# A three-block network on one core: the inverse roots of five norms are multiplied onto the matmuls' outputs, and the raw residual is fed to them tile by tile

## The chip, the cores and the metric

One core of one Trainium2 chip runs the whole network in one program. The metric is the time of one execution in device microseconds, lower is better. The engines are TensorE (PE in the views), VectorE (DVE), ScalarE (ACT), GpSimd (POOL) and SyncE (SP, which starts the transfers of weights).

## The reference

The network works on 256 tokens of width 1024 in float32; its first block prepends 16 meta tokens (272 columns). Block one: a conformer convolution (pw1, gate, depthwise convolution, layer norm, SiLU, pw2) and a SwiGLU FFN of width 2816. Block two: a pooling mix and a mixture of eight experts. Block three, twice a layer: a hybrid attention layer (input projection `w_in2`, gates, output `wo2`), then a recurrent layer (`w_in3`, `wo3`) and a second FFN. Ahead of each matmul stage stands a norm:

```python
def rms_norm(x, g):
    xf = x.astype(jnp.float32)
    y = xf * lax.rsqrt(jnp.mean(xf * xf, axis=-1, keepdims=True) + RMS_EPS)
    return y.astype(x.dtype) * g
...
def swiglu(h, w_gate, w_up, w_down):
    return (jax.nn.silu(h @ w_gate) * (h @ w_up)) @ w_down
```

The inverse root is one number per token, so it may stand before the matmul or behind it, as long as the step behind (SiLU, sigmoid) sees the scaled value.

## The kernel before

Activations lie feature-major: eight tiles of 128 features by 256 or 272 tokens. Weights come in chunks of 1 MB ([128, 2048], eight blocks of 128x256) into a ring of six slots. A float32 product is made of three: ScalarE copies a chunk to a rounded high part (L969), VectorE subtracts to get the low part (L1220), and inputs are split the same way (high on ScalarE, L989; low on VectorE, L1227). `split_pair` (L443) then issues, for each of the eight input tiles and both halves, high by high (L455), high by low (L458) and low by high (L459): 48 matmuls fill two banks of PSUM, called a pair here. Three pairs of banks go round; `bank_owner` makes TensorE wait until the values of three pairs ago have been taken out. Chunks are split three ahead of their use.

Each engine runs its own list in the order in which the code issues it, and waits on counting semaphores; nothing reorders it. ScalarE's split of a chunk waits until TensorE has begun on an earlier one (`pre_begun`, `post_begun`).

The norms are numbered 0 to 10: 0 before pw1, 1 the layer norm, 2 before FFN 0 (22 pairs, then 4 down pairs), 3 before the pooling, 4 before the router, 5 (the network's middle norm, `final_g`) and 6 before `w_in2` (24 pairs), 7 behind `wo2`, 8 before `w_in3` (21 pairs), 9 before FFN 3 (22 and 4 pairs), 10 the last one. In a norm ScalarE squares the tiles (L979), TensorE sums them over the features by a matmul with ones (`sum_squares`, L483), VectorE scales the sum and adds epsilon (L1206), ScalarE takes the root (L981), VectorE the reciprocal (`rstd`, L1209), and then VectorE, ScalarE and VectorE again make scaled input, high and low part tile by tile (L1241, L989, L1227). In the FFN, ScalarE takes SiLU of the gate's bank into `gate_sb` (L1022) and VectorE multiplies it by the other bank. In `w_in2` and `w_in3` some pairs are taken by VectorE (L1496), others by ScalarE with their function. The 24 gates per token (L703) follow pair 23 of `w_in2` and the compression (L714) follows them. GpSimd builds diagonals for the convolution (L1799) in the first 120 us and makes a few adds of 128x256 late in the program (L1804).

## Time and profile before

| | us |
|---|---|
| median of 3 runs | 2279.29 |
| lowest and highest run | 2275.84, 2280.2 |
| the profiled execution | 2278.21 |
| its span | 2276.2 |
| TensorE busy | 2134.3 (94%) |
| VectorE, ScalarE, GpSimd busy | 1522.6, 1174.8, 120.6 |
| mean granted clock of TensorE | 0.951 |

The span runs from the first to the last instruction recorded, 2 us less than the execution's time. The granted clock is given as a share of 2.4 GHz; 0.50 is the level of 1.2 GHz. A busy share is a mean over all stages.

### The profile page before, as it was taken

How to read it: one execution, taken by the hardware profiler on the slowest of the kernel's cores; microseconds unless marked ns; L12 is line 12 of the kernel's file. 1: busy time of each engine (PE TensorE's matmuls, PEld its weight loads, DVE VectorE, ACT ScalarE, POOL GpSimd, SP SyncE). 2: the span in 40 equal slices, each digit the busy share in tenths (PEclk: the TensorE clock that was granted, in tenths of full speed). 3: DMA queues.
4: the chain of work that ended last, by engine and by line, in shares of the span. 5: the costliest groups of instructions: out<-in, count | busy, mean ns of one | idle time of the engine just before them, and what ended most of it. 6: DMA issues, size and time to landing. Idle time of an engine off the chain costs nothing.

```text
span 2276.2 us, 31696 instructions
## 1 busy us (share of the span) xinstructions
PE 2134.3 (94%) x12296; PEld 1869.2 (82%) x12296; DVE 1522.6 (67%) x1697; ACT 1174.8 (52%) x1223; POOL 120.6 (5%) x170
## 2 busy tenths in 40 slices
PE   7989999699999999999999999989998899779998
PEld 6979998588888888878888888789976799658997
DVE  7865543689897988889797988864254365325553
ACT  4134432367777776777777777644243243404442
POOL 8800000000000000000000000000000000020000
PEclk9989999799999999999999999999857999889999
DMA  4214444089898989989898989835401345124541
GB/s 180 91 61 144 180 172 147 20 338 371 314 369 326 357 338 346 347 337 370 315 368 327 356 336 347 312 127 186 169 1 38 111 151 188 51 93 148 186 180 61
DMA packets 70101, 504.18 MB, mean 222 GB/s; under 512 B 7680, under 2 KB 8704, under 8 KB 8832
## 3 DMA queue, kind: packets, MB, share of 16 engines
q1 hardware_dynamic: 70016, 502.95, 59.0%
q8 instruction: 65, 1.06, 0.2%
q14 instruction: 20, 0.16, 0.0%
HBM read 501.87 MB, written 1.05 MB: 221 GB/s over the span
## 4 chain that ended last, share of the span: by engine, by line
PE 86%; DVE 7%; ACT 3%; issue 3%; DMA 0%; POOL 0%; DVEq 0%; ACTq 0%; POOLq 0%
PE ps L455 10%; PE ps L459 10%; PE ps L458 10%; PE ps L629 8%; PE ps L625 8%; PE ps L628 8%; PE ps L650 5%; PE ps L654 4%; PE ps L653 4%; PE ps L437 3%; PE ps L501 2%; PE ps L483 2%; DVE ring_r L1403 1%; PE ps L586 1%; PE ps L592 1%
## 5 line engine op out<-in xcount | busy, mean ns | idle before, releaser
L1403 DVE TENSOR_TENSOR ring_r<-ring,high 128x2048 fp32r<-128x2048 f32 x227 | 517.7, 2289 | 96.7 <-ACT high L1062 91.6
L455 PE MATMUL ps<-sq_r,high 128*128 128x256 f32 (+1 forms) x1472 | 422.4, 287 | 26.1 <-DVE scr_r L1227 26.1
L458 PE MATMUL ps<-scr_r,high 128*128 128x256 f32 (+1 forms) x1536 | 440.5, 287 | 0.0
L1062 ACT ACTIVATE high<-ring 128x2048 fp32r<-128x2048 f32 x224 | 428.5, 1913 | 18.9 <-DMA ring<-w_stream 18.6
L459 PE MATMUL ps<-sq_r,ring_r 128*128 128x256 f32 (+1 forms) x1472 | 421.1, 286 | 0.0
L1220 DVE TENSOR_TENSOR ring_r<-ring,high 128x2048 fp32r<-128x2048 f32 x120 | 274.9, 2293 | 213.7 <-ACT high L969 213.4
L628 PE MATMUL ps<-ring_r,big_r 128*128 128x512 f32 x896 | 350.0, 391 | 0.0
L969 ACT ACTIVATE high<-ring 128x2048 fp32r<-128x2048 f32 x120 | 228.8, 1909 | 153.2 <-PE ps L455 153.0
L455 PEld LDWEIGHTS ps<-sq_r,high 128*128 128x128 f32 x1472 | 281.1, 191 | 28.8 <-issue 26.5
L458 PEld LDWEIGHTS ps<-scr_r,high 128*128 128x128 f32 x1536 | 294.9, 192 | 0.2
L625 PE MATMUL ps<-high,big_r 128*128 128x512 f32 x704 | 287.2, 408 | 4.2 <-DVE ring_r L1403 4.2
L459 PEld LDWEIGHTS ps<-sq_r,ring_r 128*128 128x128 f32 x1472 | 281.6, 191 | 0.0
L629 PE MATMUL ps<-high,big_r 128*128 128x512 f32 x704 | 275.9, 392 | 0.0
L1403 DVE TENSOR_TENSOR ring_r<-ring,scr_r 128x2048 fp32r<-128x2048 f32 x112 | 254.7, 2289 | 8.0 <-ACT scr_r L1062 3.6
L1062 ACT ACTIVATE scr_r<-ring 128x2048 fp32r<-128x2048 f32 x112 | 214.3, 1914 | 16.0 <-DMA ring<-w_stream 15.5
L628 PEld LDWEIGHTS ps<-ring_r,big_r 128*128 128x128 f32 x896 | 169.1, 189 | 32.1
L653 PE MATMUL ps<-ring_r,big_r 128*128 128x512 f32 x448 | 174.5, 389 | 0.0
L625 PEld LDWEIGHTS ps<-high,big_r 128*128 128x128 f32 x704 | 132.7, 188 | 28.6 <-DVE ring_r L1403 4.4
L629 PEld LDWEIGHTS ps<-high,big_r 128*128 128x128 f32 x704 | 132.4, 188 | 28.4
L1066 ACT ACTIVATE big_r<-ps 128x256 fp32r<-128x256 f32 x112 | 43.1, 384 | 161.5 <-PE ps L636 160.9
L650 PE MATMUL ps<-scr_r,big_r 128*128 128x512 f32 x256 | 102.4, 400 | 1.6
L455 PE MATMUL ps<-big_r,high 128*128 128x272 f32 (+1 forms) x352 | 100.7, 286 | 2.0 <-ACT gate_sb L1022 2.0
(344 smaller groups left out, 3179.6 us busy)
## 6 DMA issues: line engine op xcount, KB each, us to landing
ring<-w_stream SPq DMA_DIRECT2D x477, 1024.0 KB, 4.8
h<-h_in SPq DMA_DIRECT2D x1, 1088.0 KB, 5.3
out<-hn SPq DMA_DIRECT2D x1, 1024.0 KB, 4.7
vec<-vec_in SPq DMA_DIRECT2D x1, 576.0 KB, 8.2
```

Source lines behind the costliest of these rows:

```text
L455: mm = pe.matmul(o, w_high[:, cols], x_high[:, k, 0:t], start=(k == 0), stop=False)
L458: pe.matmul(o, w_high[:, cols], x_low[:, k, 0:t], start=False, stop=False)
L459: mm = pe.matmul(o, w_low[:, cols], x_high[:, k, 0:t], start=False, stop=(k == kt - 1))
L625: mm = pe.matmul(o, x_item_high[:, k, :], w_high[:, cols], start=(k == 0), stop=False)
L628: pe.matmul(o, x_item_high[:, k, :], w_low[:, cols], start=False, stop=False)
L629: mm = pe.matmul(o, x_item_low[:, k, :], w_high[:, cols], start=False, stop=(k == KD - 1))
L650: mm = pe.matmul(o, hid_t_high[:, kk, :], w_high[:, cols], start=first, stop=False)
L653: pe.matmul(o, hid_t_high[:, kk, :], w_low[:, cols], start=False, stop=False)
L969: act.activation(parts_at(c, 0, CH)[0], blocks_at(c, 0, CH), ACT.Copy).then_inc(S["weights_high"], 1)
L1062: act.activation(w_high, w, ACT.Copy).then_inc(S["moe_high"], 1)
L1220: dve.tensor_tensor(w_low, blocks_at(c, 0, CH), w_high.bitcast(F32), ALU.subtract).then_inc(S["weights_low"], 1)
L1403: dve.tensor_tensor(w_low, w, w_high.bitcast(F32), ALU.subtract).then_inc(S["moe_low"], 1)
```

## The change

Norms 2, 5 with 6, 8 and 9 no longer scale the input by `rstd`. ScalarE copies the raw residual times the norm's weight (a pointer operand) as the high part, VectorE makes the low part in one instruction (`input_low`), and the pair of matmuls may start as soon as the first tile's parts are there. The sum of squares is issued behind pair 0 (norms 2, 8, 9) or pair 1 (norms 5, 6). Each pair's output is multiplied by `rstd` on VectorE on its way out of PSUM, and ScalarE's SiLU and sigmoids then work in place in SBUF. For the pairs whose output is token-major, two tiny matmuls turn `rstd` into a column (`turn_root`). Norms 5 and 6 share one input with the weights `gain56` = `final_g` x `pre_g`; the root of both together comes from two sums in the halves of bank 7, and `x` itself is scaled by VectorE in pairs 4 to 11.

In every norm but 0, GpSimd adds squares 0 to 5 (`sum_six`, five dependent adds), so that TensorE sums three tiles. ScalarE takes the root straight from PSUM with scale and epsilon; a small root ahead of it brings the table in. The gates and the `w_if` rows read the raw `x` with weights that GpSimd scales once; the gates move behind pair 2. The addition of the attention layer's output to `x` moves from VectorE to GpSimd. The FFN's pairs use the banks turned by one. Line numbers in the changed kernel differ: L473, L476, L477 are the three matmuls, L507 the sum of squares, L1002 and L1293 the two splits of weights.

```diff
-            def sum_squares(i, t):
-                for k in range(KD):
-                    pe.wait_ge(S["sq_ready"], 8 * i + k + 1)
-                    mm = pe.matmul(ps[:, 7, 0:t], ones[:, 0:P], sq[:, k, 0:t], start=(k == 0), stop=(k == KD - 1))
+            def sum_squares(i, t, bank=7, at=0):
+
+                if i == 0:
+                    tiles = range(KD)
+                else:
+                    tiles = (0, 6, 7)
+                    pe.wait_ge(S["sq_summed"], i)
+                for k in tiles:
+                    pe.wait_ge(*sq_at(i, k))
+                    mm = pe.matmul(ps[:, bank, at:at + t], ones[:, 0:P], squares_of(i)[:, k, 0:t],
+                                   start=(k == 0), stop=(k == KD - 1))
                 mm.then_inc(S["sum_done"], 1)
+
+            def turn_root(n):
+                pe.wait_ge(S["root_ready"], n + 1)
+                for t in range(2):
+                    mm = pe.matmul(ps[:, 6, 48 + t:49 + t], rstd[0:1, t * P:(t + 1) * P], ones[0:1, 0:1],
+                                   start=True, stop=True)
+                mm.then_inc(S["root_turned"], 1)
...
-                sum_squares(norm_i, t)
                 for p in range(KF):
-                    b = 2 * (p % 3)
-                    split_pair(b_in + p * KD, KD, in_high, x_low, t, b, S["ffn_gu"],
+                    b = 2 * ((p + 1) % 3)
+                    split_pair(b_in + p * KD, KD, sq_r, x_low, t, b, S["ffn_gu"],
                                after_split(split_n) if p == 0 else None)
-                    bank_owner[b] = (S["ffn_sig"], n * KF + p + 1)
-                    bank_owner[b + 1] = (S["ffn_mul"], n * KF + p + 1)
+                    bank_owner[b] = bank_owner[b + 1] = (S["ffn_scaled"], n * KF + p + 1)
+                    if p == 0:
+                        sum_squares(norm_i, t)
...
-                    b = 2 * (j % 3)
+                    b = 2 * ((j + 2) % 3)
...
-            pe.wait_ge(S["moe_all"], 1)
-
-
-            sum_squares(5, SEQ)
-            sum_squares(6, SEQ)
             for p in range(24):
                 b = 2 * (p % 3)
                 if p < 21:
-                    split_pair(BOFF["w_in2"] + p * KD, KD, in_high, in_low, SEQ, b, S["in2_done"],
+                    split_pair(BOFF["w_in2"] + p * KD, KD, hn_r, in_low, SEQ, b, S["in2_done"],
                                after_split(3) if p == 0 else None)
                 else:
 
-                    token_pair(BOFF["w_in2"] + p * KD, in_high, in_low, b, S["in2_done"])
-                bank_owner[b] = bank_owner[b + 1] = taken(taker2, "in2", p)
-
-            for t in range(2):
-                for k in range(KD):
-                    mm = pe.matmul(ps[:, 6, t * 24:(t + 1) * 24], hn256[:, k, t * P:(t + 1) * P],
-                                   vcol("w_gates", k * 24, 24), start=(k == 0), stop=(k == KD - 1))
-            mm.then_inc(S["gl_done"], 1)
-
-            pe.wait_ge(S["in2_act"], taker2.count("act"))
-            pe.wait_ge(S["in2_dve"], taker2.count("dve"))
+                    token_pair(BOFF["w_in2"] + p * KD, hn_r, in_low, b, S["in2_done"])
+                bank_owner[b] = bank_owner[b + 1] = (S["in2_dve"], p + 1)
+                if p == 1:
+                    sum_squares(5, SEQ)
+                    sum_squares(6, SEQ, at=SEQ)
+                if p == 2:
+                    for t in range(2):
+                        for k in range(KD):
+                            mm = pe.matmul(ps[:, 6, t * 24:(t + 1) * 24], x[:, k, t * P:(t + 1) * P],
+                                           vcol("w_gates", k * 24, 24), start=(k == 0), stop=(k == KD - 1))
+                    mm.then_inc(S["gl_done"], 1)
+                    turn_root(0)
...
+            def root(n_sums, t, eps, bank=7, at=0):
+
+                act.wait_ge(S["sum_done"], n_sums)
+                act.activation(var[:, 0:t], ps[:, bank, at:at + t], ACT.Sqrt, bias=eps, scale=1.0 / D)\
+                   .then_inc(S["std_ready"], 1)
+
+            def norm(i, src, t, ready, first_block=None, eps=eps_col, bank=7):
+
+                for k in range(KD):
+                    if first_block and k in (4, 6):
+                        split_weights(first_block // CH + k - 4)
+                    if k == KD - 2:
+                        act.activation(warm, eps_col, ACT.Sqrt)
+                    ready(k)
+                    act.activation(sq[:, k, 0:t], src[:, k, 0:t], ACT.Square).then_inc(S["sq_ready"], 1)
+                root(i + 1, t, eps, bank)
...
+            def input_parts(i, src, dst, gain, t, ready, first_block):
 
                 for k in range(KD):
                     if first_block and k in (4, 6):
                         split_weights(first_block // CH + k - 4)
                     ready(k)
-                    act.activation(sq[:, k, 0:t], src[:, k, 0:t], ACT.Square).then_inc(S["sq_ready"], 1)
-                act.wait_ge(S["var_ready"], i + 1)
-                act.activation(var[:, 0:t], var[:, 0:t], ACT.Sqrt).then_inc(S["std_ready"], 1)
-                if first_block == 0:
-                    split_weights(0)
-                if split_n is not None:
-                    for k in range(KD):
-                        if first_block == 0 and k == 3:
-                            split_weights(1)
-                        act.wait_ge(S["normed"], 8 * i + k + 1)
-                        act.activation(in_high[:, k, 0:t], hn[:, k, 0:t], ACT.Copy).then_inc(S["input_high"], 1)
-
+                    act.activation(dst[:, k, 0:t], src[:, k, 0:t], ACT.Copy, scale=gain[:, k:k + 1])\
+                       .then_inc(S["input_high"], 1)
+                    for q in (k,) if k < 6 else (6, 7) if k == 7 else ():
+                        act.activation(squares_of(i)[:, q, 0:t], src[:, q, 0:t], ACT.Square)\
...
+            input_parts(2, h, sq_r, vcol("ffn_g0", 0, 8), T0, lambda k: act.wait_ge(S["h1_ready"], k + 1),
+                        BOFF["ffn0_in"])
...
-                        act.wait_ge(S["ffn_gu"], n * 2 * KF + 2 * p + 2)
-                        if p >= 2:
-                            act.wait_ge(S["ffn_hid"], n * KF + p - 1)
-                        act.activation(gate_sb[:, p % 2, 0:t], ps[:, 2 * (p % 3), 0:t], ACT.Silu)\
+                        act.wait_ge(S["ffn_scaled"], n * KF + p + 1)
+                        act.activation(gu[:, p % 2, 0, 0:t], gu[:, p % 2, 0, 0:t], ACT.Silu)\
...
+            act.wait_ge(S["sq_summed"], 1)
+            for k in range(KD):
+                act.wait_ge(S["moe_out"], items * 4 + (k // 2 + 1))
+                act.activation(hn_r[:, k, 0:SEQ], x[:, k, :], ACT.Copy, scale=gain56[:, k:k + 1])\
+                   .then_inc(S["input_high"], 1)
+            for k in range(KD):
+                act.activation(sq[:, k, 0:SEQ], x[:, k, :], ACT.Square).then_inc(S["sq_ready"], 1)
+            for k in range(KD):
+                act.activation(squares2[:, k, 0:SEQ], x[:, k, :], ACT.Square, scale=vcol("final_g", k))\
+                   .then_inc(S["sq_ready"], 1)
+            act.wait_ge(S["var_ready"], 1)
+            act.activation(var[:, 0:SEQ], var[:, 0:SEQ], ACT.Sqrt).then_inc(S["std_ready"], 1)
+            act.wait_ge(S["root_ready"], 1)
+            root(7, SEQ, eps_col)
...
-            def inverse_root(i, t, eps):
-                dve.wait_ge(S["sum_done"], i + 1)
-                dve.tensor_scalar(var[:, 0:t], ps[:, 7, 0:t], 1.0 / D, eps, ALU.mult, ALU.add)\
-                   .then_inc(S["var_ready"], 1)
+            def inverse_root(i, t):
                 dve.wait_ge(S["std_ready"], i + 1)
...
+            def times_root(t):
+
+                return rstd[:, 0:t].unsqueeze(1).broadcast_to([P, 2, t])
...
+            def input_low(src, k, gain, t, high_part, low):
+
+                inputs_split[0] += 1
+                dve.wait_ge(S["input_high"], inputs_split[0])
+                dve.scalar_tensor_tensor(out=low[:, k, 0:t], in0=src[:, k, 0:t], scalar=gain[:, k:k + 1],
+                                         in1=high_part[:, k, 0:t].bitcast(F32), op0=ALU.mult, op1=ALU.subtract)\
+                   .then_inc(S["input_low"], 1)
...
+                if m in (4, 6):
+                    split_weights(BOFF["ffn0_in"] // CH + m - 4)
+                if m:
+                    input_low(h, m - 1, vcol("ffn_g0", 0, 8), T0, sq_r, in_low_ffn0)
+            input_low(h, KD - 1, vcol("ffn_g0", 0, 8), T0, sq_r, in_low_ffn0)
...
+                        b = 2 * ((p + 1) % 3)
+                        dve.wait_ge(S["ffn_gu"], n * 2 * KF + 2 * p + 2)
+                        if p >= 2:
+                            dve.wait_ge(S["ffn_hid"], n * KF + p - 1)
+                        dve.tensor_tensor(gu[:, p % 2, :, 0:t], ps[:, b:b + 2, 0:t], times_root(t), ALU.mult)\
+                           .then_inc(S["ffn_scaled"], 1)
                         split_weights((b_in + p * KD + KD - 1) // CH + LOOK)
                         dve.wait_ge(S["ffn_sig"], n * KF + p + 1)
-                        dve.tensor_tensor(gate_sb[:, p % 2, 0:t], ps[:, 2 * (p % 3) + 1, 0:t],
-                                          gate_sb[:, p % 2, 0:t], ALU.mult).then_inc(S["ffn_mul"], 1)
+                        dve.tensor_tensor(gu[:, p % 2, 1, 0:t], gu[:, p % 2, 0, 0:t], gu[:, p % 2, 1, 0:t], ALU.mult)\
+                           .then_inc(S["ffn_mul"], 1)
...
+                for k in (2 * n - 2, 2 * n - 1):
+                    if n:
+                        input_low(x, k, gain56, SEQ, hn_r, in_low)
+            for k in (6, 7):
+                input_low(x, k, gain56, SEQ, hn_r, in_low)
+            split_weights(BOFF["w_in2"] // CH + LOOK)
...
+                    ins = dve.scalar_tensor_tensor(out=dst, in0=ps[:, b:b + 2, 0:SEQ],
+                                                   scalar=0.125 if n < KS or QB <= n < KB else 1.0,
+                                                   in1=times_root(SEQ), op0=ALU.mult, op1=ALU.mult)
...
+                if k >= 2:
+                    input_low(x, k - 2, vcol("mix3_g", 0, 8), SEQ, hn_r, in_low)
...
+            def sum_six(i, t):
+
+                sums = squares_of(i)
+                pool.wait_ge(*sq_at(i, 0))
+                for k in range(1, 6):
+                    pool.wait_ge(*sq_at(i, k))
+                    ins = pool.tensor_tensor(sums[:, 0, 0:t], sums[:, 0, 0:t], sums[:, k, 0:t], ALU.add)
+                    if k < 5:
+                        step(ins)
+                ins.then_inc(S["sq_summed"], 1)
...
+            for i, t in ((1, T0), (2, T0), (3, T0), (4, SEQ), (5, SEQ), (6, SEQ)):
+                sum_six(i, t)
...
+            sum_six(7, SEQ)
+            for k in range(KD):
+                pool.wait_ge(S["post_scaled"], k + 1)
+                pool.tensor_tensor(x[:, k, :], x[:, k, :], zo[:, k, :], ALU.add).then_inc(S["normed"], 1)
+            sum_six(8, SEQ)
```

On VectorE at the end of pw2, before (`h<-ps` are the residual adds, `ring_r` the low part of weights, L1209 the reciprocal of norm 2):

```order
L1220 TENSOR_TENSOR ring_r<-ring,high 128x2048 [waits weights_high]
L1293 SCALAR_TENSOR_TENSOR h<-ps,vec,h 128x272 [waits pw2_done] x2
L1220 TENSOR_TENSOR ring_r<-ring,high 128x2048 [waits weights_high]
L1293 SCALAR_TENSOR_TENSOR h<-ps,vec,h 128x272 [waits pw2_done] x2
L1220 TENSOR_TENSOR ring_r<-ring,high 128x2048 [waits weights_high]
L1293 SCALAR_TENSOR_TENSOR h<-ps,vec,h 128x272 [waits pw2_done] x2
L1220 TENSOR_TENSOR ring_r<-ring,high 128x2048 [waits weights_high]
L1293 SCALAR_TENSOR_TENSOR h<-ps,vec,h 128x272 [waits pw2_done] x2
L1206 TENSOR_SCALAR var<-ps 128x272 [waits sum_done]
```

and in the changed kernel (L1306 is the low part of an input):

```order
L1293 TENSOR_TENSOR ring_r<-ring,high 128x2048 [waits weights_high]
L1372 SCALAR_TENSOR_TENSOR h<-ps,vec,h 128x272 [waits pw2_done] x2
L1306 SCALAR_TENSOR_TENSOR scr_r<-h,vec,sq_r 128x272 [waits input_high]
L1293 TENSOR_TENSOR ring_r<-ring,high 128x2048 [waits weights_high]
L1372 SCALAR_TENSOR_TENSOR h<-ps,vec,h 128x272 [waits pw2_done]
L1306 SCALAR_TENSOR_TENSOR scr_r<-h,vec,sq_r 128x272 [waits input_high]
L1372 SCALAR_TENSOR_TENSOR h<-ps,vec,h 128x272 [waits pw2_done]
L1306 SCALAR_TENSOR_TENSOR scr_r<-h,vec,sq_r 128x272 [waits input_high]
L1293 TENSOR_TENSOR ring_r<-ring,high 128x2048 [waits weights_high]
L1372 SCALAR_TENSOR_TENSOR h<-ps,vec,h 128x272 [waits pw2_done]
L1306 SCALAR_TENSOR_TENSOR scr_r<-h,vec,sq_r 128x272 [waits input_high]
```

The first low part now stands between the first two residual adds and the split and the other adds. On ScalarE at the same place, before (L979 the squares, L989 the high parts, of which each waits for a scaled tile):

```order
L969 ACTIVATE high<-ring 128x2048 [waits pre_begun,dense_landed0]
L969 ACTIVATE high<-ring 128x2048 [waits pre_begun,dense_landed1]
L969 ACTIVATE high<-ring 128x2048 [waits pre_begun,dense_landed2]
L979 ACTIVATE sq<-h 128x272 [waits h1_ready] x8
L981 ACT_TABLE_LOAD
L981 ACTIVATE var<-var 128x272 [waits var_ready]
L989 ACTIVATE sq_r<-hn 128x272 [waits normed] x8
L969 ACTIVATE high<-ring 128x2048 [waits pre_begun,dense_landed3]
```

and in the changed kernel:

```order
L1002 ACTIVATE high<-ring 128x2048 [waits pre_begun,dense_landed5]
L1002 ACTIVATE high<-ring 128x2048 [waits pre_begun,dense_landed0]
L1002 ACTIVATE high<-ring 128x2048 [waits pre_begun,dense_landed1]
L1002 ACTIVATE high<-ring 128x2048 [waits pre_begun,dense_landed2]
L1028 ACTIVATE sq_r<-h,vec 128x272 [waits h1_ready]
L1031 ACTIVATE big<-h 128x272
L1028 ACTIVATE sq_r<-h,vec 128x272 [waits h1_ready]
L1031 ACTIVATE big<-h 128x272
```

The four splits keep their place, and the high parts of the inputs (L1028) with their squares (L1031) come right behind them.

On TensorE in `w_in2`, in the changed kernel, behind pair 1 (L507 the sums of norms 5 and 6, L733 the gates):

```order
L476 MATMUL ps<-scr_r,high 128x256
L477 MATMUL ps<-hn_r,ring_r 128x256
L507 MATMUL ps<-sq,ones 128x256 [waits sq_ready,sq_summed]
L507 MATMUL ps<-sq,ones 128x256 [waits sq_ready] x2
L507 MATMUL ps<-big,ones 128x256 [waits sq_ready,sq_summed]
L507 MATMUL ps<-big,ones 128x256 [waits sq_ready] x2
L437 REGISTER_ALU
L473 MATMUL ps<-hn_r,high 128x256 [waits moe_low]
```

and behind pair 2:

```order
L476 MATMUL ps<-scr_r,high 128x256
L477 MATMUL ps<-hn_r,ring_r 128x256
L733 MATMUL ps<-vec,x 128x24 x16
L514 MATMUL ps<-ones,rstd 128x1 [waits root_ready]
L514 MATMUL ps<-ones,rstd 128x1
L473 MATMUL ps<-hn_r,high 128x256 [waits weights_low,in2_dve]
L476 MATMUL ps<-scr_r,high 128x256
```

Before, the sixteen sums stood ahead of pair 0 and the gates behind pair 23:

```order
L483 MATMUL ps<-sq,ones 128x256 [waits sq_ready,moe_all]
L483 MATMUL ps<-sq,ones 128x256 [waits sq_ready] x15
```

Both moved into the stage, and pair 0 is the first thing behind the last MoE sum.

## Rows read from the trace of the kernel before

**Rows 1.** The page's part 4, chain that ended last, by engine.
```profile
PE 86%; DVE 7%; ACT 3%; issue 3%; DMA 0%; POOL 0%; DVEq 0%; ACTq 0%; POOLq 0%
```

**Rows 2.** Waits of TensorE: us in total, times, longest.
```profile
PE ps L455 <- DVE scr_r L1227: 31.5, 7, 7.0
...
PE ps L483 <- ACT sq L979: 18.7, 6, 6.6
...
PE ps L455 <- ACT gate_sb L1022: 2.0, 2, 1.0
```

**Rows 3.** Timeline about norm 2: start, us, [idle before]; last row: clock third from end.
```profile
168.43 1.92 ACT L969 ACTIVATE high<-ring 128x2048 fp32r<-128x2048 f32 x1 [4.08 <-PE ps L455]
...
177.92 0.44 DVE L1206 TENSOR_SCALAR var<-ps 128x272 f32<-128x272 f32 x1 [3.12 <-PE ps L483]
178.85 1.85 DVE L1209 RECIPROCAL rstd<-var 128x272 f32<-128x272 f32 x1 [0.50 <-ACT var L981]
...
182.44 0.56 PE L455 MATMUL ps<-sq_r,high 128*128 128x272 f32 x1 [4.56 <-DVE scr_r L1227]
...
190.79 0.40 ACT L1022 ACTIVATE gate_sb<-ps 128x272 f32<-128x272 f32 x1 [0.81 <-PE ps L459]
...
196.79 0.40 ACT L1022 ACTIVATE gate_sb<-ps 128x272 f32<-128x272 f32 x1 [3.80 <-PE ps L459]
...
182.00:187.00 5.00, 4.56 (x20) 4.59 (x21) 4.86 (x14) 2.82 (x8) 0.00 (x0) 0.50 0.51 182
```

**Rows 4.** Timeline about norms 5 and 6, TensorE, then VectorE.
```profile
1476.32 1.99 PE L592 MATMUL ps<-big 128*128 128x256 f32 x8 [0.78 <-DVE x L1430]
...
1496.85 0.38 PE L455 MATMUL ps<-sq_r,high 128*128 128x256 f32 x1 [4.26 <-DVE scr_r L1227]
...
1510.02 0.69 DVE L1496 TENSOR_SCALAR big<-ps 128x512 f32<-128x512 f32 x1 [1.25 <-PE ps L459]
...
1515.68 0.68 DVE L1491 COPY h<-ps 64x512 f32<-64x512 f32 x1 [1.25 <-PE ps L459]
```

**Rows 5.** GpSimd: a group (busy, mean ns), and timeline beside VectorE's.
```profile
L1804 POOL TENSOR_TENSOR hn<-scr 128x256 f32<-128x256 f32 x8 | 5.6, 724 | 1657.5 <-DVE scr L1575 1657.5
...
49.96 3.49 POOL L1799 TENSOR_SCALAR big<-ident,vec 128x128 f32<-128x128 f32 x6
...
49.55 8.34 DVE L1262 SCALAR_TENSOR_TENSOR big<-big,vec 128x272 f32<-128x272 f32 x15
...
57.81 3.28 POOL L1799 TENSOR_SCALAR big<-ident,vec 128x128 f32<-128x128 f32 x2
...
58.34 2.28 DVE L1220 TENSOR_TENSOR ring_r<-ring,high 128x2048 fp32r<-128x2048 f32 x1
```

**Rows 6.** Timeline of norm 1, ScalarE and VectorE.
```profile
137.76 2.90 ACT L979 ACTIVATE sq<-big 128x272 f32<-128x272 f32 x8 [24.54 <-DVE big L1281]
...
143.15 1.85 DVE L1209 RECIPROCAL rstd<-var 128x272 f32<-128x272 f32 x1 [0.50 <-ACT var L981]
```

**Rows 7.** Gates and compression on TensorE, timeline and granted clock.
```profile
1634.47 3.88 PE L703 MATMUL ps<-vec,hn 128*128 128x24 f32 x32
1638.17 13.86 PE L714 MATMUL ps<-h,ring 128*128 128x45 f32 x64
...
1638.00:1640.00 2.00, 2.00 (x11) 2.00 (x11) 0.00 (x0) 0.21 (x1) 0.00 (x0) 0.50 0.11 25
```

**Rows 8.** Timeline about norms 7, 8 and 9.
```profile
1815.08 1.75 DVE L1209 RECIPROCAL rstd<-var 128x256 f32<-128x256 f32 x1 [0.48 <-ACT var L981]
...
1828.49 0.35 PE L455 MATMUL ps<-sq_r,high 128*128 128x256 f32 x1 [4.38 <-DVE scr_r L1227]
...
2062.17 3.62 PE L483 MATMUL ps<-sq,ones 128*128 128x256 f32 x16
...
2078.14 0.39 ACT L1022 ACTIVATE gate_sb<-ps 128x256 f32<-128x256 f32 x1 [0.61 <-PE ps L459]
```

**Rows 9.** A group of VectorE, two banks taken from PSUM.
```profile
L1496 DVE TENSOR_SCALAR big<-ps 128x512 f32<-128x512 f32 x4 | 2.8, 692 | 5.1 <-PE ps L459 5.1
```

245 lines of the change are left out of this document (150 added, 95 removed).

## The prediction

> **What bounds the kernel now.** I read the chain that ended last first: TensorE carries 86% of it [rows 1], so a change is worth what it takes out of TensorE's waits and its own instructions. The waits of TensorE came next [rows 2]. Seven first matmuls of a stage wait for the low part of an input (`scr_r`, L1227), 31.5 us in all; the sums of squares (L483) wait for squares of ScalarE, 18.7 us over six norms; two 1.0-us waits for a bank stand before the down projections. These are the norms, and each has one anatomy, seen in norm 2 [rows 3]: eight tiles of squares are summed, then VectorE's variance (177.92), ScalarE's root, the reciprocal (178.85, 1.85 us), the scaled input, its high and low part, and at 182.44 the first matmul. Pair 0 of the FFN is done when ScalarE takes it at 190.79; the next is taken at 196.79, so a pair of banks of 272 columns costs 6.0 us at full clock, and pair 0 took 8.3: the granted clock was 0.50 (the 1.2 GHz level) from 182 to 187, after TensorE had stood idle. A bubble therefore costs its length and some 2 us behind it. A pair of 256 columns costs 5.67 us (1510.02 to 1515.68) [rows 4].
>
> **The change, place by place** (minus is faster; made against the profiled execution, 2278.2 us, 1.1 under the median).
>
> Sums and roots. TensorE sums three tiles in place of eight: 3.62 us [rows 8] x 3/8 = 1.4. The variance instruction goes from the chain: sum to reciprocal falls from 0.93 to about 0.5. Where the squares were long ready this is plain profit: norm 3 -2.5, norm 10 -2.2, norm 0 (only the variance) -0.4. The other five squares must be added on GpSimd first, each add waiting for the one before. GpSimd's 128x256 add takes 725 ns [rows 5]; with its semaphore step I take 0.80, 0.85 at 272 columns. In norm 1 the squares start at 137.76, 0.36 apart [rows 6], so five adds end at 138.5 + 4.3 = 142.8; the sum ends at 144.2 to 144.8 and the reciprocal starts at 144.7 to 145.3 where it was 143.15. That is +2.0, a loss. Norm 4 has the same form and its squares come at one go: +1.9.
>
> Norm 2. TensorE could start pair 0 at once, but VectorE's order stops that. Its instruction for the low part of tile 0 stands behind the first two residual adds and ahead of the split of the next weights and of the other six adds, and waits for ScalarE's copy, which stands behind all four weight splits; the last of those runs 168.43 to 170.35 [rows 3]. So VectorE is idle from about 157.4, where the second add of that step ends now, to 170.9. What is queued behind: three splits (2.29 each [rows 5]), six adds and eight low parts (0.44 to 0.5 each), together 13.1 us, so the last low part lands at 184.0. TensorE follows at the low clock; its last tile takes six matmuls, about 1.35, then the sum 1.4 to 2.0: pair 1 starts at 187.4, and it was 190.7. So -3.3, where without the queueing it would have been about -9.
>
> FFN banks turned by one pair: the down stage's first bank is free. The two waits go: -2.0 [rows 2].
>
> Norms 5 and 6, and the gates. Before, the last MoE sum ends at 1478.3 and pair 0 of `w_in2` starts at 1496.85. Now copies and low parts come tile by tile behind each `x` sum, so pair 0 starts at 1478.4. To the start of pair 3: three pairs 17.0, two sums 2.8, the gates 3.9 [rows 7], 1502.0 in all, against 1515.6 [rows 4]: -13.6. The roots are in time: squares of both norms end at about 1487, GpSimd's two chains at 1491, the reciprocal at 1497, and the first take is needed at 1502. The gates' 3.9 us are gone at the end of the stage. The compression (L714) ran wholly at the 0.50 clock behind them, 13.86 us [rows 7]; behind full pairs its first microseconds may run at 2.4 GHz, -1.9. Against that: the last pair's take (0.69, [rows 9]) is exposed, +0.9; the narrow gates may drop the clock in mid-stage as they did before L714 (from 1638 it was 0.50), which costs 2.1; GpSimd meeting one split, +1. Sum -13.6 - 3.9 - 1.9 + 0.9 + 2.1 + 1.0 = -15.4.
>
> Norms 7 and 8. The root of norm 7 is there 1.8 us earlier than 1815.08 [rows 8]. The `x` adds move to GpSimd (eight of 0.72) and feed tile by tile; pair 0 starts at 1817.5, was 1828.49. It ends at about 1823.4, but the sum of norm 8 needs GpSimd's five adds behind its eight: 1826.2, and a split of VectorE falls into them, 1 more. Pair 1 starts at 1828.7, against 1835.9 (1828.49, 5.67, and 1.7 of low clock): -7.2.
>
> Norm 9. The last `wo3` matmul ends at 2062.3. Inputs 0 to 5 are ready by then, and 6 and 7 by 2065. Pair 0 ends at 2068.0, the sum at 2069.4, where pair 1 started at 2078.0 (taken at 2078.14 [rows 8]): -8.6.
>
> Takes. Every pair is now multiplied by VectorE from PSUM: 0.69 us [rows 9], taking as long as the plain take of the same shape. In the FFNs a pair then costs it 2.29 + 0.75 + 2 x 0.44 = 3.9 of 6.0 us; in `w_in2` 2.29 + 0.69 + 0.48 for the scaling of `x` = 3.5 of 5.67. Hidden behind TensorE's pair, so nothing. The moved SiLU runs behind it and a bank is wanted only two pairs later. Without that cover each microsecond would count about eighty times.
>
> **Sum:** -0.4 + 2.0 - 3.3 - 2.0 - 2.5 + 1.9 - 15.4 - 7.2 - 8.6 - 2.2 = -37.7; 2278.2 - 37.7 = 2240.5, or 2241.6 at the level of the median.
>
> **What GpSimd's adds cost** no row shows beside such work, so it is bounded. Lower end: 0.80 for each. Upper: a GpSimd instruction that meets a weight split (L1220) waits it out; two took 3.28 us from 57.81 while the split ran from 58.34, where two alone take 1.2: one hold is 2.1 us. Short VectorE instructions did no such thing: from 49.96 six took 3.49 while fifteen of L1262 ran [rows 5]. I take 0.80 with one hold, charged above where a split is near and the chain is late. The Trainium skill ("SBUF — State Buffer", Who interferes with whom) says that a VectorE instruction with two SBUF inputs and a GpSimd instruction reading SBUF exclude each other for the whole of an instruction. The hold beside the split agrees; by the rule the short low parts would block too, and the chains of norms 1, 7 and 8 would be some 2 us longer each, for a sum of about -32. The six short ones do not show that, so I keep my price.
>
> **Rivals.**
> A, as summed: 2242, its own range 2235 to 2250. Chance 0.58.
> B, GpSimd is late. Each of the six chains whose end TensorE waits for or nearly waits for (norms 1, 2, 5 with 6, 7, 8, 9) meets one or two more holds of 2.1: 6 x 2.1 = +12.6, 2254. For it: splits follow one another in the norms' stretches; against it: three of these chains have 2 to 4 us of slack. 0.16, of which 0.05 for the milder form in which only the short low parts block (three chains, +2 each, 2248).
> C, the clock. The broken feeding of pair 0 (norms 2, 8) and the narrow matmuls in mid-stage leave TensorE at 1.2 GHz for longer; each further stretch like 182 to 187 costs 2 to 3, four of them +10: 2252. 0.10.
> D, more gain: TensorE working where it used to idle keeps the full clock at four norms and the gates cost no clock, -8: 2233. 0.06.
> E, slower. VectorE becomes the bound in the scaled stages: each bank is freed only by its take, and the take stands behind a split that waits for ScalarE, which itself waits for the take (SiLU, then copy, then split). If that ring lost over 0.5 us in each of some eighty pairs, the 38 us would be gone; at 0.7 it ends at 2297. Against it: 2 us of slack a pair. 0.07.
> F, the waits only move: what is started earlier waits for splits that come no sooner, 2278. Against it: the weights for pairs 0 to 3 were split ahead. 0.03.
>
> Under 0.2% a measurement of this kernel tells nothing from no change. A to D are faster, 0.90; F the same, 0.03; E slower, 0.07. The range 2230 to 2257 holds A, D and the larger part of B and C.
>
> **What the profile after would show.** The waits of first matmuls for `scr_r` fall from 31.5 to under 12 us; what stays is norm 2, fed in steps until about 184, and norm 0. VectorE idle for some 13 us in front of one low part near 157. Sums of three tiles; the reciprocals of norms 1 and 4 later by 2, of 3 and 10 earlier. Pair 0 of `w_in2` right behind 1478 less what was won before. GpSimd's adds at 0.80 apart, with single ones of about 3 beside splits. The prediction is wrong if pairs in mid-stage wait for a bank, if sums wait for `sq_summed` over 3 us each, or if the half clock holds through pair 1.

## The result, and the profile after

| | before | changed |
|---|---|---|
| median of the runs, us | 2278.32 | 2256.18 |
| lowest and highest, us | 2275.84, 2280.2 | 2254.49, 2256.97 |
| profiled execution, us | 2278.21 | 2255.49 |

The ratio is 0.9907 (95% interval 0.9895 to 0.9919): faster by 0.9%, where 1.6% was forecast. Applied to the 2279.29 of before that the prediction had, it gives 2258.1, one microsecond outside the range. Two later sets of runs of the same kernel gave 0.9868 (0.9850 to 0.9886) and 0.9874 (0.9858 to 0.9889), which is 2249 and 2251 and inside the range. Which side of the range's end the kernel fell on was thus a matter of the set; that it gained less than was summed holds for all three.

The waits of TensorE in the changed kernel (in all, times, longest), to be read against [rows 2]:

```profile
PE ps L507 <- POOL sq L1877: 14.1, 3, 6.6
...
PE ps L473 <- DVE scr_r L1300: 13.2, 3, 6.7
...
PE ps L473 <- DVE scr_r L1306: 9.7, 4, 5.2
...
PE ps L507 <- ACT sq L1019: 8.9, 4, 7.8
```

The waits of first matmuls for low parts fell from 31.5 to 22.9 us (forecast: under 12). The forecast named norms 0 and 2; norm 1 waits 5.0 as well and norm 8 5.2. The two waits for `gate_sb` are gone. A new releaser stands at the top, GpSimd's sums, 14.1 us: 6.6 at norm 1, 5.4 at norm 4, 2.0 at norm 8. Two of them are over the 3 us that the prediction had named as a sign of being wrong. With the 8.9 us for ScalarE's squares, the waits of the sums grew, from 18.7 to 23.

To place the difference I compare the start of ScalarE's splits of dense weight chunks (L969 before, L1002 after; 120 in each kernel, in the same order). They follow TensorE's progress, so a shift that grows or shrinks between two of them belongs to the stretch between. Differences to before in us, worked out from the starts in the timelines, for three profiled executions of the same changed kernel. The last column is the kernel before with nothing but the FFN's banks turned (an experiment below): outside the two turns and the stretches of norm 2 and FFN 3, which hold the FFN's pairs, its code is that of before, so it shows how far two executions of one code lie apart:

| stretch | forecast | first | second | third | banks alone |
|---|---|---|---|---|---|
| norm 0, to the first split | -0.4 | +1.3 | +2.1 | +0.7 | +1.1 |
| first pairs of pw1 | 0 | +2.6 | +1.3 | +0.4 | +1.0 |
| convolution, norm 1 | +2.0 | +2.3 | +1.8 | +3.8 | -2.2 |
| norm 2 | -3.3 | -1.1 | -2.5 | -1.0 | -0.5 |
| turn to the down stage of FFN 0 | -1.0 | -2.1 | -2.1 | -2.1 | -1.2 |
| norms 3 and 4, and the MoE | -0.6 | +0.6 | +3.6 | +0.8 | +2.7 |
| norms 5 and 6, `w_in2` to attention's end | -15.4 | -14.9 | -20.4 | -19.7 | -3.0 |
| norms 7 and 8 | -7.2 | -3.7 | -5.3 | -3.7 | +1.0 |
| rest of `w_in3` | 0 | +1.9 | +1.9 | +1.9 | 0.0 |
| recurrent layer | 0 | +2.4 | +0.4 | +0.2 | +0.2 |
| norm 9 | -8.6 | -8.6 | -8.6 | -8.6 | 0.0 |
| rest of FFN 3 with its down turn | -1.0 | -1.5 | -1.5 | -1.5 | -0.7 |
| norm 10 | -2.2 | -2.1 | -2.1 | -2.1 | 0.0 |
| sum | -37.7 | -22.8 | -31.3 | -30.9 | -1.7 |

In the FFNs a split stands some 1 us later in ScalarE's list than it did (behind a wait for VectorE's multiplication), which the row of norm 2 carries and the row of the turn gives back: by TensorE's own rows pair 1 went from 190.60 to 194.79 and the first down matmul from 317.77 to 320.99, so norm 2 won 2.1 in the first execution and the turn 1.0.

The last column warns of single rows. In norm 0, the first pairs, the convolution, the MoE and attention the one execution of the kernel before differs from the other by 1.0 to 4.7 us with the same code, so a row of that size says little there; for these places I go by durations inside the stretch. The turns, norms 9 and 10 and the rest of `w_in3` repeat to 0.1 us.

**Norm 0**, the timeline of ScalarE and TensorE in the changed kernel (start, us):

```profile
5.95 1.28 ACT L1019 ACT_TABLE_LOAD   x1 [5.95 <-DMA h<-h_in]
7.24 2.03 ACT L1019 ACTIVATE sq<-h 128x272 f32<-128x272 f32 x6
9.29 1.28 ACT L1017 ACT_TABLE_LOAD   x1
10.58 0.20 ACT L1017 ACTIVATE small<-small 128x1 f32<-128x1 f32 x1
10.69 0.73 ACT L1019 ACTIVATE sq<-h 128x272 f32<-128x272 f32 x2
...
20.54 0.57 PE L473 MATMUL ps<-sq_r,high 128*128 128x272 f32 x1 [6.70 <-DVE scr_r L1300]
```

and in the kernel before:

```profile
0.76 1.28 ACT L979 ACT_TABLE_LOAD   x1 [0.76 <-PEq L1925]
6.05 2.66 ACT L979 ACTIVATE sq<-h 128x272 f32<-128x272 f32 x8 [4.00 <-DMA h<-h_in]
```

The table for the squares is now loaded at 5.95, when the input has landed; before it was in place since 2.0. A second load and the small root (10.58) stand in front of the last two squares. The first matmul moved from 18.97 to 20.54. The reason is in the code: an added wait for `ones_ready` (a semaphore of the constant ones) ahead of the one for the input. The Trainium skill ("ScalarE: Activation LUTs", Step-by-step: what each stage is for) says that a load is placed right before the activation that needs it; the trace agrees, and here that is behind both waits. Before, with one wait in front, the load ran at 0.76, long before the square.

**Norm 1**, GpSimd's chain, TensorE's sum and VectorE's reciprocal:

```profile
141.39 4.61 POOL L1877 TENSOR_TENSOR sq<-sq 128x272 f32<-128x272 f32 x5 [10.86 <-ACT sq L1019]
...
146.05 3.09 PE L507 MATMUL ps<-sq,ones 128*128 128x272 f32 x6 [6.61 <-POOL sq L1877]
...
149.70 1.85 DVE L1274 RECIPROCAL rstd<-var 128x272 f32<-128x272 f32 x1 [5.14 <-ACT var L1008]
```

Five adds take 4.61 us (forecast 4.3); the three-tile sum behind the 6.6 us of waiting takes 3.09, not 1.4. Before, sixteen instructions took 3.93 while the squares arrived; now six take 3.09, at the granted clock of 0.50. From the first square to the reciprocal it is 5.39 us before and 9.27 now, the same to 0.02 us in all seven profiled executions with this sum. Norm 4 repeats it with a sum of 2.93; from its first square to the reciprocal it is 8.32 us in the same seven executions, where the kernel before took 5.13 and its version with turned banks 7.17.

**Norm 2**, VectorE, GpSimd and TensorE:

```profile
177.09 0.50 DVE L1306 SCALAR_TENSOR_TENSOR scr_r<-h,vec,sq_r 128x272 fp32r<-128x272 f32 x1 [13.14 <-ACT sq_r L1028]
177.50 2.29 DVE L1293 TENSOR_TENSOR ring_r<-ring,high 128x2048 fp32r<-128x2048 f32 x1
...
178.25 2.16 POOL L1877 TENSOR_TENSOR big<-big 128x272 f32<-128x272 f32 x1 [32.25 <-ACT big L1031]
181.22 0.96 POOL L1877 TENSOR_TENSOR big<-big 128x272 f32<-128x272 f32 x1 [0.81 <-ACT big L1031]
181.46 2.87 DVE L1293 TENSOR_TENSOR ring_r<-ring,high 128x2048 fp32r<-128x2048 f32 x1
...
182.44 2.50 POOL L1877 TENSOR_TENSOR big<-big 128x272 f32<-128x272 f32 x1 [0.26 <-POOL big L1877]
...
193.61 1.54 PE L507 MATMUL ps<-big,ones 128*128 128x272 f32 x6
194.79 0.49 PE L473 MATMUL ps<-sq_r,high 128*128 128x272 f32 x1
```

The wait of 13.14 us before the first low part is the one forecast (13.5). New is that a weight split takes 2.87 us where it took 2.29. Which engine waits goes by who began: the split of 177.50 began with no add under way and kept its 2.29, and the add inside it took 2.16; the split of 181.46 began while the add of 181.22 ran and took 2.87, and the next add 2.50. In the first and in the second execution alike, two splits began during an add and took 2.85 to 2.87, and four began before one and took 2.28 or 2.29. Pair 1 starts at 194.79, 4.2 later than before, with 6.3 brought along.

**Norms 5 and 6**, TensorE:

```profile
1480.10 1.99 PE L624 MATMUL ps<-big 128*128 128x256 f32 x8 [0.78 <-DVE x L1521]
1481.74 0.47 PE L473 MATMUL ps<-hn_r,high 128*128 128x256 f32 x1
...
1493.28 1.46 PE L507 MATMUL ps<-sq,ones 128*128 128x256 f32 x6
1494.94 1.56 PE L507 MATMUL ps<-big,ones 128*128 128x256 f32 x6 [0.21 <-POOL big L1877]
...
1502.02 3.65 PE L733 MATMUL ps<-vec,x 128*128 128x24 f32 x32
1505.60 0.60 PE L514 MATMUL ps<-ones,rstd 1*128 1x1 f32 x4
```

Pair 0 follows the last MoE sum without a gap, both sums stand behind pair 1, the gates at 1502.02, as forecast. From the end of the last MoE sum to the end of the compression it is 158.7, 157.4 and 158.8 us in the three executions, 173.7 before: -15.0, -16.3 and -14.9, where -15.4 was forecast. The last row is the four matmuls that turn the root, 0.60 us, which my sum left out.

**Norms 7 and 8**, VectorE, TensorE and GpSimd; this answers to [rows 8]:

```profile
1806.73 0.94 DVE L1697 SCALAR_TENSOR_TENSOR big<-big,vec,rstd 128x256 f32<-128x256 f32 x1
...
1807.06 0.55 PE L473 MATMUL ps<-hn_r,high 128*128 128x256 f32 x1 [5.20 <-DVE scr_r L1306]
...
1807.75 0.91 POOL L1945 TENSOR_TENSOR x<-x,big 128x256 f32<-128x256 f32 x1 [0.36 <-DVE big L1697]
...
1813.69 4.21 POOL L1877 TENSOR_TENSOR sq<-sq 128x256 f32<-128x256 f32 x5
...
1817.96 2.93 PE L507 MATMUL ps<-sq,ones 128*128 128x256 f32 x6 [2.04 <-POOL sq L1877]
```

The first matmul of `w_in3` is 10.3 us nearer to the norm, as forecast (11). But VectorE's scaling of `zo` takes 0.94 where it took 0.48, GpSimd's adds 0.91 where they took 0.72, pair 0 is fed once in 1.27 us and takes 8.9 us, and then the sum waits 2.04 for GpSimd and runs 2.93 (at the granted clock of 0.50; behind the same wait it took 1.56 in the second execution, at 1.00).

### The profile page after: what moved, and what is told of

It is laid out like the page before. It is cut to its first block, busy times and chain, and to the rows that moved or that the text cites. A ratio compares the mean times of both kernels' runs of the same rounds, so it can differ in the third digit from the quotient of the medians.

```text
span 2253.4 us, 31698 instructions
## 1 busy us (share of the span) xinstructions
PE 2115.6 (94%) x12204; PEld 1852.2 (82%) x12204; DVE 1552.3 (69%) x1726; ACT 1183.1 (53%) x1233; POOL 183.8 (8%) x247
## 4 chain that ended last, share of the span: by engine, by line
PE 85%; DVE 7%; ACT 3%; issue 3%; POOL 1%; DMA 0%; DVEq 0%; ACTq 0%; POOLq 0%
PE ps L476 10%; PE ps L473 10%; PE ps L477 10%; PE ps L657 8%; PE ps L661 8%; PE ps L660 8%; PE ps L682 5%; PE ps L686 4%; PE ps L685 4%; PE ps L455 2%; PE ps L533 2%; PE ps L618 1%; PE ps L823 1%; PE ps L624 1%; PE ps L844 1%
## 5 line engine op out<-in xcount | busy, mean ns | idle before, releaser
L476 PE MATMUL ps<-scr_r,high 128*128 128x256 f32 (+1 forms) x1536 | 441.7, 288 | 0.0
L1113 ACT ACTIVATE high<-ring 128x2048 fp32r<-128x2048 f32 x224 | 428.6, 1913 | 16.4 <-DMA ring<-w_stream 16.3
L1293 DVE TENSOR_TENSOR ring_r<-ring,high 128x2048 fp32r<-128x2048 f32 x120 | 275.7, 2299 | 122.5 <-ACT high L1002 122.4
L1002 ACT ACTIVATE high<-ring 128x2048 fp32r<-128x2048 f32 x120 | 228.3, 1905 | 138.9 <-PE ps L473 138.9
L476 PEld LDWEIGHTS ps<-scr_r,high 128*128 128x128 f32 x1536 | 295.4, 192 | 0.5
L473 PE MATMUL ps<-sq_r,high 128*128 128x272 f32 (+1 forms) x832 | 241.4, 290 | 13.2 <-DVE scr_r L1300 8.2
L477 PE MATMUL ps<-sq_r,ring_r 128*128 128x272 f32 (+1 forms) x832 | 239.8, 288 | 0.0
L473 PE MATMUL ps<-hn_r,high 128*128 128x256 f32 (+1 forms) x704 | 202.4, 287 | 10.5 <-DVE scr_r L1306 5.5
L477 PE MATMUL ps<-hn_r,ring_r 128*128 128x256 f32 (+1 forms) x704 | 200.6, 285 | 0.0
L473 PEld LDWEIGHTS ps<-sq_r,high 128*128 128x128 f32 x832 | 159.5, 192 | 14.9 <-issue 7.1
L477 PEld LDWEIGHTS ps<-sq_r,ring_r 128*128 128x128 f32 x832 | 159.1, 191 | 0.0
L1877 POOL TENSOR_TENSOR sq<-sq 128x256 f32<-128x256 f32 (+1 forms) x35 | 31.5, 900 | 1495.3 <-ACT sq L1142 1071.5
```

What stands on the lines that cost most here:

```text
L473: mm = pe.matmul(o, w_high[:, cols], x_high[:, k, 0:t], start=(k == 0), stop=False)
L476: pe.matmul(o, w_high[:, cols], x_low[:, k, 0:t], start=False, stop=False)
L477: mm = pe.matmul(o, w_low[:, cols], x_high[:, k, 0:t], start=False, stop=(k == kt - 1))
L1002: act.activation(parts_at(c, 0, CH)[0], blocks_at(c, 0, CH), ACT.Copy).then_inc(S["weights_high"], 1)
L1113: act.activation(w_high, w, ACT.Copy).then_inc(S["moe_high"], 1)
L1293: dve.tensor_tensor(w_low, blocks_at(c, 0, CH), w_high.bitcast(F32), ALU.subtract).then_inc(S["weights_low"], 1)
```

## The experiments

Ratios are to the kernel before, run beside each. The second and third set of the changed kernel are the level for the others. The four single edits (norm 0, eight-tile sums, norm 2's order, `x` adds) ran on another chip than either set, so their whole times are compared over the ratios alone, and what they show stands in their traces.

| run | median, us | ratio (95%) |
|---|---|---|
| changed, second | 2246.99 | 0.9868 (0.9850 to 0.9886) |
| changed, third | 2248.38 | 0.9874 (0.9858 to 0.9889) |
| norm 0's table early | 2250.77 | 0.9879 (0.9852 to 0.9906) |
| eight-tile sums, norms 1, 4, 8 | 2238.38 | 0.9823 (0.9807 to 0.9839) |
| norm 2's order | 2244.31 | 0.9857 (0.9837 to 0.9877) |
| `x` adds on VectorE | 2246.27 | 0.9869 (0.9846 to 0.9891) |
| first three together | 2231.47 | 0.9790 (0.9776 to 0.9803) |
| all four | 2228.18 | 0.9776 (0.9762 to 0.9789) |
| sums on TensorE but in norm 3 | 2250.67 | 0.9871 (0.9856 to 0.9887) |
| kernel before, banks turned | 2276.09 | 0.9984 (0.9975 to 0.9993) |
| takes by ScalarE, unscaled | 2251.72 | 0.9885 (0.9869 to 0.9901) |

**Norm 0's table.**

```diff
             act.wait_ge(S["ones_ready"], 1)
+            act.activation(warm, eps_col, ACT.Square)
             act.wait_ge(S["h_landed"], 16)
...
-                    if k == KD - 2:
+                    if i and k == KD - 2:
```

> Norm 0 alone: a tiny square is issued ahead of the wait for the input, so ScalarE's table is there when the input lands, and the small root between the squares is left out of norm 0. Theory (table load behind the wait costs 1.3 us, the small root 1.5, and TensorE then spends the whole first pair at the 0.50 clock): the reciprocal of norm 0 starts by 12.8 where it was 14.51, the first matmul by 18.9 where it was 20.54, the clock is back before 25, and everything behind is 3 to 4 us earlier, about 2252.5. Rival (the start was late for another reason, and only the clock's luck cost the rest): within 1 us of the changed kernel, 2256.

```profile
0.76 1.28 ACT L1035 ACT_TABLE_LOAD   x1 [0.76 <-PEq L2069]
2.06 0.20 ACT L1035 ACTIVATE small<-small 128x1 f32<-128x1 f32 x1
6.00 2.67 ACT L1019 ACTIVATE sq<-h 128x272 f32<-128x272 f32 x8 [3.74 <-DMA h<-h_in]
...
19.43 0.57 PE L473 MATMUL ps<-sq_r,high 128*128 128x272 f32 x1 [6.78 <-DVE scr_r L1301]
```

The eight squares run in one go at 6.00 and the first matmul starts at 19.43, 1.1 us earlier than in the changed kernel's first execution (I had said 1.6 or more). One pair of executions would not show it, since the sum of the same sixteen instructions takes 5.3 to 6.9 us. Over all traces, the first matmul stands at 19.05 to 19.83 in the three kernels with the early table and at 20.02 to 21.19 in the eight without: 1.0 us between the means. The small root costs nothing here, as the sum ends 2.4 us behind the last square anyway. The rest of the theory fell: the first pairs still lost 1.0 here, against 0.4 in the third execution of the changed kernel itself. The time is within the scatter of the changed kernel.

**Eight-tile sums.**

```diff
-                if i == 0:
+                if i not in SUMMED:
                     tiles = range(KD)
...
+                if i not in SUMMED:
+                    return
                 sums = squares_of(i)
```

`SUMMED` holds all norms but 0, 1, 4 and 8.

> Norms 1, 4 and 8 sum all eight tiles on TensorE again, GpSimd adds nothing there. Theory (a three-tile sum behind an idle wait for GpSimd runs at the low clock, 2.93 to 3.09 us, and the chain is 4 to 4.6): norm 1 gives back 3.6 us, norm 4 1.5, norm 8 1 to 2, together -6 to -7, about 2249.5. Rival (GpSimd's chains cost little, the loss is VectorE's feeding): norm 1 and 4 within 1 us of now, total -2 or less, 2254 or more.

```profile
137.87 3.02 PE L508 MATMUL ps<-sq,ones 128*128 128x272 f32 x12 [1.47 <-ACT sq L1020]
141.47 1.18 PE L508 MATMUL ps<-sq,ones 128*128 128x272 f32 x4 [0.58 <-ACT sq L1020]
```

TensorE sums the squares as they come and is done at 142.6. From the first square to the reciprocal norm 1 takes 5.82 us where it took 9.27: 3.45 us, the expected 3.6. It stays 0.4 over before, with the small root and its table load between the squares. Norm 4 takes 6.95 from its first square to the reciprocal, not 8.32: 1.4 us, as expected (1.5), though its sixteen instructions ran partly at the low clock and took 5.9. Norm 8 went to -5.5, against -3.7 to -5.3. These three are 5 to 7 us; the kernel stands 9 us under its level, and the rest is in stretches whose clock differs.

**Norm 2's order.**

```diff
             for j in range(4):
                 split_weights((BOFF["pw2"] + j * KD + KD - 1) // CH + LOOK)
-            input_parts(2, h, sq_r, vcol("ffn_g0", 0, 8), T0, lambda k: act.wait_ge(S["h1_ready"], k + 1),
-                        BOFF["ffn0_in"])
+                if j:
+                    input_parts(2, h, sq_r, vcol("ffn_g0", 0, 8), T0, lambda k: act.wait_ge(S["h1_ready"], k + 1),
+                                0, (2 * j - 2, 2 * j - 1))
+            input_parts(2, h, sq_r, vcol("ffn_g0", 0, 8), T0, lambda k: act.wait_ge(S["h1_ready"], k + 1),
+                        0, (6, 7))
```

> ScalarE's copies of tiles 0 to 5 in norm 2 stand right behind the weight splits of pw2's pairs and no longer behind all four, so VectorE is not held in front of the first low part. Theory (the order of the lists is the cost in norm 2): VectorE's wait of 13 us falls under 3, pair 0 of the FFN runs right behind pw2 without holes, pair 1 starts 6 to 7 us earlier: about 2249.5. Rival (GpSimd holding VectorE's splits, 2.87 for 2.29, and the late sum are the cost): pair 1 gains 2 or less, 2254 or more.

```profile
161.64 0.50 DVE L1309 SCALAR_TENSOR_TENSOR scr_r<-h,vec,sq_r 128x272 fp32r<-128x272 f32 x1 [0.59 <-ACT sq_r L1028]
...
182.90 1.54 PE L507 MATMUL ps<-big,ones 128*128 128x272 f32 x6
...
184.07 0.49 PE L473 MATMUL ps<-sq_r,high 128*128 128x272 f32 x1
```

VectorE's first low part comes 0.59 us behind its adds, not 13.14. From the end of pw2 (177.06) to pair 1 at 184.07 it is 7.0 us, where the changed kernel took 14.3 in its first execution and 12.9 in its second, and the kernel before 16.4. The gain is 7.3 or 5.9 us, about the expected 6 to 7. Part of it belongs to the rival: here no split begins while an add runs, so the two holds of 0.58 us are gone with the wait. The whole was to be 2249.5 by the old level; by the new one it is 3 to 4 us under it, with a spread of 2237.8 to 2249.2.

**The additions to `x` on VectorE.**

```diff
+                if 1 <= k <= KD:
+                    dve.wait_ge(S["post_scaled"], k)
+                    dve.tensor_tensor(x[:, k - 1, :], x[:, k - 1, :], zo[:, k - 1, :], ALU.add)\
+                       .then_inc(S["normed"], 1)
```

and the loop on GpSimd is gone.

> In norm 8 the eight additions to x are on VectorE again, GpSimd makes only the sums. Theory (VectorE and GpSimd hold each other: L1697 takes 0.95 for 0.48 beside GpSimd's adds, which take 0.90): L1697 is back at 0.48 and VectorE's round of three instructions takes about 1.3 a tile as now; the gain is in the sum of squares, which no longer stands behind eight adds: pair 1 of w_in3 0.5 to 1.5 us earlier, about 2255. Rival (the adds are slow on GpSimd by themselves, nothing holds VectorE): L1697 stays above 0.8 and pair 0 gets slower, 2257.

The group of L1697 in this kernel (busy, mean ns), then in the changed one:

```profile
L1697 DVE SCALAR_TENSOR_TENSOR big<-big,vec,rstd 128x256 f32<-128x256 f32 x8 | 4.2, 536 | 0.0
```

```profile
L1697 DVE SCALAR_TENSOR_TENSOR big<-big,vec,rstd 128x256 f32<-128x256 f32 x8 | 6.5, 832 | 0.0
```

So most of what L1697 took over 0.48 us (482 ns in the kernel before) was the doing of GpSimd's adds to `x`. GpSimd's sums still hold VectorE:

```profile
1803.87 1.60 POOL L1881 TENSOR_TENSOR sq<-sq 128x256 f32<-128x256 f32 x2 [12.32 <-ACT sq L1031]
...
1804.80 0.95 DVE L1702 TENSOR_TENSOR x<-x,big 128x256 f32<-128x256 f32 x1
```

Five of VectorE's short instructions take 0.95 in place of 0.42 to 0.48 beside them. The sum's wait for GpSimd is gone and the stretch of norms 7 and 8 went to -5.6. The time is that of the changed kernel: the runs cannot tell a gain of 1 us.

**The changed kernel again**, with no edit.

> The changed kernel itself, beside the next three on their chip. In the four runs before it the clock's phases in the sparse stages (attention, recurrent layer) took up to 5 us more or less for the same work. Theory (the changed kernel stands where its first runs put it): median 2254 to 2258. Rival (its first runs fell into unlucky phases of the clock): median 2247 to 2252, two clusters some 8 us apart.

The runs are 2246.99, 2243.88, 2255.24, 2249.51 and 2246.48, so the theory fell: the kernel does not stand at 2254 to 2258. With the third set, below, the changed kernel has 13 runs: seven from 2243.9 to 2249.5, six from 2254.5 to 2257.0, none between. I read two levels some 8 us apart, with the first set four times on the upper one, where the later sets were twice in nine. That this was chance, and not the first set's chip, is not shown. The same stretch of attention, in windows of 5 us (busy time and instructions of TensorE, its weight loads, VectorE, ScalarE and GpSimd, then the granted clock, the DMA share and GB/s), in the first profiled execution:

```profile
1733.00:1738.00 5.00, 3.79 (x23) 2.81 (x22) 0.42 (x1) 1.12 (x2) 0.00 (x0) 0.50 0.01 3
1738.00:1743.00 5.00, 5.00 (x14) 3.99 (x13) 0.00 (x0) 0.00 (x0) 0.00 (x0) 0.53 0.54 210
1743.00:1748.00 5.00, 5.00 (x25) 4.41 (x24) 1.01 (x4) 0.00 (x0) 0.17 (x1) 1.00 0.00 0
```

and in this one:

```profile
1733.00:1738.00 5.00, 3.80 (x29) 3.00 (x28) 0.43 (x1) 1.19 (x2) 0.00 (x0) 0.89 0.01 3
1738.00:1743.00 5.00, 5.00 (x25) 4.41 (x24) 0.00 (x0) 0.00 (x0) 0.00 (x0) 1.00 0.57 210
1743.00:1748.00 5.00, 5.00 (x25) 4.39 (x24) 1.42 (x4) 0.00 (x0) 1.41 (x2) 1.00 0.59 185
```

TensorE waits for the same things in both, to a tenth of a us, but from 1733 to 1743 one runs at the lower level and the other mostly at the higher. From the end of the compression to the end of attention the first lost 0.1 us on the kernel before, the second won 4.2 and the third 4.8. The kernel with only its banks turned, whose attention is untouched, won 4.7: the slow attention is that of the kernel before's one trace, and of the first execution.

**Three mended, and four.** The edits above for norm 0, the sums of norms 1, 4 and 8, and norm 2's order in one kernel, then the additions to `x` as well.

> Norm 0's early table, norm 2's order, and the eight-tile sums of norms 1, 4 and 8 together. Theory (three separate losses, each on the path of TensorE): they add, 3 + 7 + 7 us under the changed kernel beside it, 2233 to 2238. Rival (what is won in one place is lost to the clock in the next): under 10 us, above 2241.

> As the one before, with norm 8's additions to x on VectorE too. Theory (without GpSimd's sums in norm 8, the additions on GpSimd are all that holds VectorE there: L1697 0.95 for 0.48): pair 0 of w_in3 is fed every 1.3 to 1.4 us a tile either way, so within 1 us of the kernel before it in this list. Rival (the mutual hold is a loss that VectorE alone does not have): 2 us less than it.

2231.47 is 15.5 us under the second set of the changed kernel, run beside it: the rival (under 10) is out, and the losses add. Between the two profiled executions 1.3 us of it stand before the convolution, 3.5 at norm 1, 5.9 at norm 2, and norm 4 takes 4.73 from square to reciprocal, 3.6 less. What is left over is in stretches whose clock differs, in both directions. The fourth edit gave 3.3 us in the median, with ranges that overlap (2227.4 to 2233.5, 2224.3 to 2233.4), and 0.3 in the stretch of norm 8; that it helps is not shown. The kernel with all four edits is the fastest of the study, 2.2% under the kernel before.

**All sums on TensorE.** The edit of the eight-tile sums with `SUMMED` holding norm 3 alone:

```diff
+SUMMED = [3]
```

> Every norm but 3 sums its eight tiles on TensorE; GpSimd adds no squares there. Theory (GpSimd's sums are worth their place only where the squares lie ready long before): norms 1, 4 and 8 give 3.6, 1.5 and 1 to 2, norm 2 gets its splits back at 2.29 (-1.2) and pays 2.1 for the sum, norms 5 and 6 pay 4, 7, 9 and 10 pay 2 each: 1 to 5 us slower than the changed kernel beside it. Rival (holding VectorE is the main cost of the sums): 3 us or more faster than it.

```profile
173.51 0.50 DVE L1307 SCALAR_TENSOR_TENSOR scr_r<-h,vec,sq_r 128x272 fp32r<-128x272 f32 x1 [13.16 <-ACT sq_r L1029]
...
177.78 2.28 DVE L1294 TENSOR_TENSOR ring_r<-ring,high 128x2048 fp32r<-128x2048 f32 x1
```

VectorE's first low part still comes after the same wait, but its splits are back at 2.28 us: the 2.87 was GpSimd's doing. The median is 3.7 us above the second set of the changed kernel, less than the two differ within themselves (the ratios are 0.9871 and 0.9868), so the whole decides between neither theory nor rival. By stretches, against that set's profiled execution, it loses 2.4 at norm 2, 2.3 at norms 5 and 6 and 2.1 at norm 9, and wins 2.9 at norm 1: where squares are ready early, GpSimd's sums pay, and where they are waited for, they cost.

**Banks alone.**

```diff
-                    b = 2 * (p % 3)
+                    b = 2 * ((p + 1) % 3)
...
-                    b = 2 * (j % 3)
+                    b = 2 * ((j + 2) % 3)
```

> The kernel before with one part of the change alone: the FFN's pairs and down pairs use the banks turned by one. Theory (the down stage's first bank was the whole of the two waits of 1.0 us): both waits are gone and the time falls by 2.0 us, ratio 0.9991. Rival (the first down pair waits for the last hidden tile instead): the waits move to a low part of the hidden values, no change.

The waits for `gate_sb` are gone and each turn to a down stage is 1.2 us shorter. The ratio, 0.9984 (0.9975 to 0.9993), holds the expected 0.9991.

**Plain takes.** The curved pairs wait for `in3_done` and ScalarE reads `ps`. The kernel leaves out the inverse root in these fourteen pairs, so its values are not the reference's; VectorE makes a tiny memset for each in place of the take.

```diff
-                act.wait_ge(S["in3_dve"], p + 1)
-                act.activation(proj[:, 2 * p:2 * p + 2, :], proj[:, 2 * p:2 * p + 2, :],
+                act.wait_ge(S["in3_done"], 2 * p + 2)
+                b = 2 * (p % 3)
+                act.activation(proj[:, 2 * p:2 * p + 2, :], ps[:, b:b + 2, 0:SEQ],
```

> The changed kernel, but fourteen pairs of w_in3 are taken from PSUM by ScalarE with their function, as before the change, and not multiplied by the inverse root (left out there, so these values are not the reference's). Theory (each pair taken and multiplied by VectorE slows TensorE by some hundredths of a us, since from the third to the eighteenth split of w_in3 the stage took 87.2 us where it took 85.3): the stage is back at 85.3 to 85.6. Rival (another input buffer or the order of the lists does it): it stays at 87.

The stretch took 86.4 us, not the expected 85.3 to 85.6: 1.1 over before where it was 1.9. Its later part (ten chunks) fell from +1.0 to +0.3, its first five stayed at +0.8; there stand the matmuls that turn the root, 0.60 us. So the theory holds for 0.8 of 1.9; no run leaves out the turn.

**The changed kernel, third time**, with no edit.

> The changed kernel a third time, as the level for its neighbours. Theory (phases of the clock in the sparse stages decide between two levels): runs near 2245 and near 2254, nothing between for long, the difference in attention and in the recurrent layer. Rival (the chips differ): all runs at one level.

2247.4, 2248.9, 2247.9 and 2255.0. Runs at both levels are there again, on another chip than the second set's, so the levels are not the chips'.

## Why the prediction was off

The direction and six of the ten terms held (the banks, norms 3, 5 with 6, 9, 10, and norm 2 in most executions); the sum was 37.7 where the three profiles give 22.8, 31.3 and 30.9. What failed is the step "what GpSimd's adds cost", with the sum of three tiles priced at 1.4 us at full clock, and the terms put at nothing: the table load in norm 0, the turn of the root and the takes, and the clock. Part of the first set's distance is luck of the clock, which the range did not hold. By its own steps:

- "Norm 0 (only the variance) -0.4" failed in sign. I looked at what left the chain, not at what was put in front of it. It measured +0.7 to +2.1; 1.0 of it is the table load behind the added wait (shown by the kernels with the early table). The first pairs added 0.4 to 2.6, but 1.0 also in the kernel with only its banks turned: that is the clock and not the change.
- Norm 1, "+2.0, a loss": the loss is 3.9 at the norm itself (9.27 for 5.39 us), since the three-tile sum took 3.09, not 1.4 to 2.0. A price at full clock (3.62 x 3/8) was put behind a wait after which the clock was at 0.50; the second experiment gives 3.45 of it back. That the row shows less is the clock in the convolution: from pw1 to the first square it is 25.1 us in the trace of before and 23.5 in the kernel with its banks turned.
- Norm 2, "-3.3": by TensorE's rows -2.1 in the first execution and -3.5 in the second. The order's cost was read rightly and shown by the third experiment. What was missing is that GpSimd holds two of VectorE's splits, 0.58 us each.
- The turned banks, -2.0: right.
- Norms 3 and 10: right (-2.5 and -2.2 were said; -2.3 and -2.1). Norm 4, "+1.9": by the first matmul behind it +1.6, which looks right by luck. From its first square to its reciprocal it takes 8.32 us in every execution of the changed kernel, where code of before takes 5.13 or 7.17: +3.2 or +1.2. Its sum ran at the low clock like norm 1's, 2.93.
- The MoE behind norm 4 has no term. It lost 1.3, 2.5 and 1.5 us in the three executions, but 1.5 also in the kernel with only its banks turned, so most of that is not the change.
- Norms 5 and 6 and the gates, "-15.4": right, -14.9 to -16.3 up to the end of the compression, with pair 0 without a gap and the gates in mid-stage. The -20.4 and -19.7 of the table are 4 to 5 us of clock in attention on top, that the change did not win.
- Norms 7 and 8, "-7.2": -3.7 to -5.3. The feeding was right and the price wrong: the adds cost 0.90 and VectorE 0.94 for 0.48, so pair 0 took 8.9 us for 5.9; the sum came late, and slow in the first execution. I had weighed the rule on the shared port against one row of short instructions and let the row win. That row was of 128x128 multiplications with one SBUF tile, 0.60 us each, beside VectorE's L1262, which went from 0.50 to 0.54. The runs decide for the rule of the Trainium skill ("SBUF — State Buffer", Who interferes with whom), and in the direction that I had not priced at all: VectorE waits as well.
  The trace of before had it too, 25 us ahead of the row that I took. The same instructions of GpSimd, first beside the short L1241 and L1227, then with VectorE idle or on instructions with one input:

```profile
24.41 3.49 POOL L1799 TENSOR_SCALAR big<-ident,vec 128x128 f32<-128x128 f32 x4
...
24.76 0.60 DVE L1241 SCALAR_TENSOR_TENSOR hn<-h,vec,rstd 128x272 f32<-128x272 f32 x1
...
10.00 4.08 POOL L1799 TENSOR_SCALAR big<-ident,vec 128x128 f32<-128x128 f32 x7 [0.34 <-DMA vec<-vec_in]
```

  Four took 3.49 us, 0.87 each, where seven took 4.08, 0.58 each; and L1241 took 0.60 for 0.50.
- Norm 9, "-8.6": right.
- "Hidden behind TensorE's pair, so nothing": nearly. `w_in3` lost 1.9 us in every execution. 0.8 of it are the takes, by the experiment; 0.6 would be the four matmuls for the turned root, that I left out. What is left, and the 1.2 us that `w_in2` loses in the same way, was not tested.
- No term for the clock in stages that the change does not touch. Attention behind the compression and the recurrent layer differ by 5 and 2 us between executions of one kernel, the compression itself by 2.9 (12.5 and 9.6 us). The range should have held that; I had three runs of the kernel before, 4.4 apart, and took them for its whole width.

Rival B (GpSimd late) and C (the clock) together describe the miss; each got its chance as if alone. B is right in its cause and not in its form: it had more holds of GpSimd behind splits, where the runs show VectorE held as well and the sums at the low clock. Why the changed kernel falls on the upper level in some executions stays open: the windows show that the clock differs for the same waits, not why.

## What to carry to other kernels

When work moves to GpSimd, price both engines: where VectorE's instruction has two SBUF inputs, the one that began while the other engine's ran was the one that grew. Look at every row that has the two engines side by side, not at one. A short piece of TensorE's work behind a long wait is to be priced at the low clock (3.09 us for 1.54 behind 6.6 us of waiting), so shrinking it while lengthening the wait may lose. Where inputs are fed tile by tile, check the order of the lists: the first low part waited 13 us for a copy that stood behind all the splits, and moving it won 5.9 to 7.3 us, where the whole change had won 2.1 to 3.5 at that norm. And before a row of differences is read, profile the old code twice: here it differed from itself by up to 4.7 us in one stretch.

## What was not expected of the hardware

The runs of the same kernel fell into two groups some 8 us apart (2244 to 2250, and 2254 to 2257), both of them on each of two chips, with the same waits and another granted clock in its sparse stages. Where an add of GpSimd and a split of VectorE overlap, the one that begins second grows: the split to 2.86 us for 2.28 when an add is under way, the add to 2.2 to 2.7 us when it begins inside a split, which then keeps its 2.28.
